# Leaving empty places out of gather and store, and storing expert rows by token

## The chip, the cores and the metric

The kernel runs on one core of one Trainium2 chip. The metric is the device time of one execution in microseconds (us). All tensors are float32.

## The reference

A two layer backbone (D_MODEL 1024) runs over 128 context tokens and 256 latent tokens, 384 in all. Each layer has attention, a recurrent branch, and a mixture of experts (MoE). Only the last is touched by the change:

```python
scores = jax.nn.sigmoid(t.astype(F32) @ router_w.astype(F32))     # 16 experts in 4 groups
...                                                               # best group, top 2 experts in it
_, e_idx = lax.top_k(jnp.where(in_grp, sel, -jnp.inf), TOP_K)
...
gates = jnp.sum(jax.nn.one_hot(e_idx, N_EXPERTS, dtype=F32) * w_sel[..., None], axis=1)
gu = jnp.einsum('td,edf->tef', t, w_gate_up)                      # (1024, 2*512) per expert
g_, u_ = jnp.split(gu, 2, axis=-1)
act = jax.nn.silu(g_) * u_ * gates[..., None].astype(t.dtype)
return jnp.einsum('tef,efd->td', act, w_down).reshape(B, S, D)    # (512, 1024) per expert
```

Every token picks two of 16 experts, so there are 768 pairs of token and pick in a layer, 48 for an expert on average. The result of a token is the sum over its two picks, each scaled by its gate.

## The kernel before

Five engines run instruction streams of their own, written out by hand and tied by semaphores (`S(name)`). SyncE (SP) issues all weight loads in the order of `CHUNKS`. ScalarE (ACT), VectorE (DVE), TensorE (PE) and GpSimd (POOL) each follow the same order of work.

**Routing.** When a layer's attention part is over, the normalized rows of all tokens are stored to `h2_rows` in DRAM. VectorE works out for each pair of token and pick its expert's block (`blk`) and its row in the block (`row`, 0 to CAP-1 with CAP = 128). `hot_c` is the one-hot of the row, `hot_b` the one-hot of the block times the token's number. TensorE multiplies the two (L748), which gives `ids`: for each place of each block the token that sits in it. Empty places hold 0, so they gather row 0. There are 16 blocks, one for each expert, and MORE = 5 blocks for experts with more than 128 rows. In the runs here no such block is needed; its branches are tested and passed over.

**The expert stage.** POOL gathers 128 rows of `h2_rows` for expert e into `xg[e % 2]` (L1878, an indirect DMA); from e = 2 it first waits until the rows of expert e-2 have been turned. TensorE turns them (`xturn`, L756), ScalarE and VectorE copy them as a high and a low part (L1178, L1756). The weights of an expert come in six pieces of 1 MiB (L446), four for gate and up, two for down. ScalarE makes the high part of a piece (`piece_high`, L1173) and VectorE the low part (`piece_low`, L1750, a subtraction of two SBUF tensors). TensorE multiplies them in `split_piece` (L785), 12 matmuls a piece. Its order in an iteration is

```python
gu(e)            # 48 matmuls
xturn(e + 1)     # needs row_gathered of e + 1
dn(e - 1)        # 24 matmuls
aturn(e)         # turns the activated rows, L822
```

ScalarE copies the result of expert e-2 out of PSUM into `yo` (`copy_y`, L1197) in iteration e, after it has made piece 3 of gate and up, and issues the plain store of its 128 rows to `expert_rows` (`store_y`, L1202). `yo` has two buffers.

**The tail.** When the last stores have landed, ScalarE signals `experts_done`. POOL then gathers the rows of each token and pick back (L1903): three tiles of 128 tokens, two picks, six indirect DMAs of 512 KB, with the places `posu = blk * 128 + row`. TensorE adds the two picks of a tile with diagonal matrices of gates (`combined`, L867). SP waits until all six are back (`back{t}`) before it goes on to the next layer's weights.

**The start.** VectorE clears `zrow`, and POOL stores it five times to the rows of the extra blocks (L1851), since the combining gather may name any row. ScalarE issues some 25 small loads; L936 is the last of them, and its first computation (L940) follows.

Of the kernel before, what the change touches and what calls it, by code (L numbers as in the profile page):

```python
# [7 lines left out]
F32 = mybir.dt.float32  # L8
F32R = mybir.dt.float32r
U32 = mybir.dt.uint32  # L10
# [22 lines left out]
CAP = 128  # L33

# [140 lines left out]
def build(nc, x_prompt, x_sample, cache_k, cache_v, state_h, c, c_ctx, norm1_g, norm2_g, w_ada, b_ada,  # L175
# [4 lines left out]
    with ctx:  # L180
# [44 lines left out]
        tokid = con[:, 1174:1177]  # L225
        num_e = con[:, 1177:1193]
        num_b = con[:, 1193:1193 + BLOCKS]
        num_c = con[:, 1193 + BLOCKS:1193 + BLOCKS + CAP]
        sel_e = con[:, 1193 + BLOCKS + CAP:1193 + BLOCKS + CAP + NE]
# [72 lines left out]
        zrow = gbf[:, 2048:3072]  # L302
# [15 lines left out]
        yd = nc.dram_tensor("expert_rows", (BLOCKS * CAP, D), F32, kind="Internal").ap()  # L318
# [18 lines left out]
        def t_free(g):  # L337
            return S(f"tbank_read{T_AT[g] % 2}")
# [69 lines left out]
        def _(sy):  # L408
# [9 lines left out]
            def more_blocks(l):  # L418
# [3 lines left out]
                for b in range(MORE):  # L422
                    with sy.If(more > b):
# [6 lines left out]
                        sy.wait_ge(S(f"x_y_ready{l}"), b + 1)  # L430
                        row = (NE + b) * CAP
                        sy.dma_start(yd[row:row + CAP, :], yo[0][0:CAP, :]).then_inc(S(f"x_stored{l}"), 16)
# [3 lines left out]
                sy.nop().then_inc(S("blocks_over"), 1)  # L436

            for n, (l, name) in enumerate(CHUNKS):
# [467 lines left out]
        def _(ac):  # L906
# [56 lines left out]
            for l in range(DEPTH):  # L963
# [243 lines left out]
                for e in range(NE):  # L1207
# [7 lines left out]
                    if e >= 2:  # L1215
                        store_y(e - 2)
# [13 lines left out]
                store_y(NE - 2)  # L1230
                copy_y(NE - 1)
                store_y(NE - 1)
# [61 lines left out]
        def _(ve):  # L1294
# [11 lines left out]
            ve.memset(zrow, 0.0)  # L1306
# [95 lines left out]
            for l in range(DEPTH):  # L1402
# [20 lines left out]
                def low_part(at):  # L1423
# [3 lines left out]
                    if l == 0 and at == 2:  # L1427
                        ve.wait_ge(S("rows_zero"), 16 * MORE)
# [292 lines left out]
                for i in range(2 * TT):  # L1721
                    pick, t = divmod(i, TT)
                    ins = ve.tensor_scalar(hot_b[:, i, :], num_b, blk[:, pick, t:t + 1], tokid[:, t:t + 1],
                                           ALU.is_equal, ALU.mult)
                ins.then_inc(S("hot_ready"), 1)
                link(ve.scalar_tensor_tensor(posu[:, :, :], blk, float(CAP), row, ALU.mult, ALU.add))
# [232 lines left out]
```

## Time and profile before

| | us |
|---|---|
| median of 3 runs | 1651.53 |
| lowest, highest | 1651.22, 1652.94 |
| the profiled execution | 1651.6 |
| its span | 1649.4 |
| TensorE busy | 1504.6 (91%) |
| VectorE busy | 1111.5 (67%) |
| ScalarE busy | 913.8 (55%) |
| GpSimd busy | 147.5 (9%) |

The span runs from the first to the last recorded instruction; the execution's own time has 2.2 us more around it. Busy times are shares over stages with different limits. The expert stages lie at about 514 to 820 us (layer 0) and 1309 to 1616 us (layer 1). Start times in the views are counted from the start of the span.

### The profile page before, as it was taken

What the parts mean: (1) busy time and instruction counts of PE and PEld (TensorE: products, weight loads), DVE (VectorE), ACT (ScalarE), POOL (GpSimd) and SP (SyncE); (2) the same over time, 40 slices, a digit from 0 to 9 for tenths busy, and PEclk for the clock granted to TensorE, in tenths of its full rate; (3) what the DMA queues carried; (4) which work ended last, traced back from release to release, by engine and by line L of the source; (5) the groups of instructions that cost most, each with busy time, mean ns of one, the idle gap of its engine ahead of it and who ended that gap; (6) DMA issues with size and microseconds to landing.
All of it is one profiled execution on the core that took longest, in us unless ns stands there. A gap on an engine that the chain in (4) does not pass through costs nothing.

```text
span 1649.4 us, 19719 instructions
## 1 busy us (share of the span) xinstructions
PE 1504.6 (91%) x7483; PEld 1219.5 (74%) x7483; DVE 1111.5 (67%) x1715; ACT 913.8 (55%) x1149; POOL 147.5 (9%) x214
## 2 busy tenths in 40 slices
PE   4899999989995999999859999998998499999996
PEld 2499876669864788888657988665988378888876
DVE  3436657764546999999652565766564679999983
ACT  1223569972222787778521345899221467877771
POOL 0100012200011100000040000221000200000001
PEclk9799999989996999999979999999999699999998
DMA  9455432225554999999463554113341589999963
GB/s 345 153 201 196 172 106 83 89 68 189 204 209 168 361 402 407 411 410 397 180 233 109 204 195 163 60 60 107 103 153 48 226 295 409 410 408 406 411 265 131
DMA packets 133876, 377.23 MB, mean 229 GB/s; under 512 B 9352, under 2 KB 12816, under 8 KB 133776
## 3 DMA queue, kind: packets, MB, share of 16 engines
q1 hardware_dynamic: 113600, 326.04, 52.7%
q0 software_dynamic: 11152, 27.80, 4.6%
q10 hardware_dynamic: 9024, 22.03, 3.4%
q8 instruction: 65, 1.06, 0.3%
q14 instruction: 35, 0.29, 0.1%
HBM read 351.19 MB, written 24.66 MB: 228 GB/s over the span
## 4 chain that ended last, share of the span: by engine, by line
PE 83%; DVE 8%; ACT 4%; issue 2%; ACTq 1%; POOL 1%; DMA 0%; DVEq 0%; POOLq 0%
PE bank L785 33%; PE bank L496 23%; PE bank L485 10%; PE bank L506 3%; PE bank L679 2%; PE bank L867 2%; PE bank L756 1%; PE bank L522 1%; PE bank L515 1%; PE bank L652 1%; PE bank L589 1%; PE bank L584 1%; PE bank L822 1%; POOL hT L1858 1%; DVE hyb L1400 1%
## 5 line engine op out<-in xcount | busy, mean ns | idle before, releaser
L785 PE MATMUL bank<-piece_high,ga_r 128*128 128x512 f32 x1536 | 492.8, 402 | 11.7 <-DVE ga_r L1756 7.8
L1750 DVE TENSOR_TENSOR spot_low<-spot,piece_high 128x2048 fp32r<-128x2048 f32 x192 | 435.8, 2288 | 44.1 <-ACT piece_high L1173 40.4
L1173 ACT ACTIVATE piece_high<-spot 128x2048 fp32r<-128x2048 f32 x192 | 367.1, 1917 | 51.7 <-PE bank L785 50.5
L785 PEld LDWEIGHTS bank<-piece_high,ga_r 128*128 128x128 f32 x1536 | 288.4, 191 | 77.2 <-DVE ga_r L1756 9.1
L785 PE MATMUL bank<-spot_low,ga_r 128*128 128x512 f32 x768 | 305.5, 398 | 0.0
L485 PE MATMUL bank<-hT,ring 128*128 128x384 f32 x576 | 196.3, 495 | 19.4 <-POOL hT L1858 12.1
L496 PE MATMUL bank<-parts_r,ga_r 128*128 128x384 f32 x768 | 202.7, 345 | 0.0
L485 PEld LDWEIGHTS bank<-hT,ring 128*128 128x128 f32 x576 | 108.5, 193 | 90.8 <-issue 20.0
L785 PEld LDWEIGHTS bank<-spot_low,ga_r 128*128 128x128 f32 x768 | 146.5, 191 | 34.1
L496 PEld LDWEIGHTS bank<-parts_r,ga_r 128*128 128x128 f32 x768 | 138.3, 188 | 5.9 <-issue 5.0
L496 PE MATMUL bank<-parts_r,gb_r 128*128 128x384 f32 x384 | 129.7, 338 | 0.0
L496 PE MATMUL bank<-parts_r,hT_r 128*128 128x384 f32 x432 | 98.3, 354 | 9.0 <-DVE parts_r L1421 9.0
L1431 DVE TENSOR_TENSOR gb_r<-ring,ga_r 128x1024 fp32r<-128x1024 f32 x48 | 58.5, 1222 | 51.5 <-ACT ga_r L979 49.9
L496 PEld LDWEIGHTS bank<-parts_r,hT_r 128*128 128x128 f32 x432 | 80.6, 197 | 12.7 <-DVE parts_r L1421 10.8
L1878 POOL DMA_INDIRECT gr<-h_rows,ids x32 | 42.5, 1330 | 485.7 <-PE bank L756 435.4
L979 ACT ACTIVATE hT_r<-ring 128x1024 fp32r<-128x1024 f32 x32 | 33.9, 1058 | 77.4 <-PE bank L496 77.4
L1871 POOL DMA_DIRECT2D gatew<-in_lru_wa x64 | 33.8, 534 | 478.6 <-PE bank L679 478.4
L496 PEld LDWEIGHTS bank<-parts_r,gb_r 128*128 128x128 f32 x384 | 72.1, 188 | 0.0
L1178 ACT ACTIVATE ga_r<-bank 128x1024 fp32r<-128x1024 f32 x32 | 32.9, 1027 | 42.8 <-PE bank L756 42.8
L949 ACT ACTIVATE tmp<-bank 128x512 f32<-128x512 f32 x24 | 14.4, 599 | 75.0 <-PE bank L506 75.0
L1858 POOL TENSOR_SCALAR hT<-hT,modA,modT 128x128 f32<-128x128 f32 x32 | 23.3, 744 | 364.1 <-DVE hT L1407 312.5
L506 PE MATMUL bank<-ring,cpad 128*32 128x512 f32 x384 | 51.1, 656 | 0.0
(283 smaller groups left out, 2227.1 us busy)
## 6 DMA issues: line engine op xcount, KB each, us to landing
spot<-in_w_gate_up SPq DMA_DIRECT2D x128, 1024.0 KB, 8.0
spot<-in_w_down SPq DMA_DIRECT2D x64, 1024.0 KB, 8.1
ring<-in_w_ada SPq DMA_DIRECT2D x24, 2048.0 KB, 8.2
ring<-in_w_in SPq DMA_DIRECT2D x22, 2048.0 KB, 8.0
expert_rows<-gb ACTq DMA_DIRECT2D x32, 512.0 KB, 7.0
ring<-in_w_attn_proj SPq DMA_DIRECT2D x4, 2048.0 KB, 8.3
ring<-in_w_rnn_proj SPq DMA_DIRECT2D x4, 2048.0 KB, 7.9
ring<-in_w_out SPq DMA_DIRECT2D x4, 2048.0 KB, 7.9
```

The costliest lines, as they stand in the source:

```text
L485: mm = pe.matmul(bank[:, 0:width], slot_kn(slot)[:, k, n * P:(n + 1) * P], rhs(k), start=(k == 0), stop=(k == KT - 1))
L496: mm = pe.matmul(bank[:, 0:T], w[:, k, :], x[:, k, :], start=(k == 0 and i == 0), stop=(k == KT - 1 and i == 2))
L506: mm = pe.matmul(bank[g:g + 32, :], cpad[:, k, :], slot_kn(s)[:, k, :], start=(k < 4), stop=(k >= 4), tile_position=(0, g))
L679: pe.matmul(bank[:, 0:CW], gatew[:, which, n % 2, :], xc[:, j, :], start=True, stop=True).then_inc(S("gemm_done"), 1)
L785: mm = pe.matmul(out[n], x[:, 2 * q + k, :], w[:, k, cols], start=(q == 0 and k == 0 and i == 0), stop=(q == pieces - 1 and k == 1 and i = ...
L979: ac.activation(w_part(kind, n)[0], slot_kn(s)[:, :, n % 4 * P:(n % 4 + 1) * P], ACT.Copy)\
L1173: ac.activation(highs[p % HIGHS], spots[u], ACT.Copy).then_inc(S("piece_high"), 1)
L1431: ve.tensor_tensor(low, slot_kn(s)[:, :, n % 4 * P:(n % 4 + 1) * P], high.bitcast(F32), ALU.subtract)\
L1750: ve.tensor_tensor(spots_low[u], spots[u], highs[p % HIGHS].bitcast(F32), ALU.subtract)\
L1858: po.tensor_scalar(hT[:, k, 0:CTX], hT[:, k, 0:CTX], modA[:, which, k, 0:1], modT[:, which * 24 + k, 0:1], ALU.mult, ALU.add).then_inc(S(" ...
L1871: po.dma_start(gatew[half * 64:half * 64 + 64, which, n % 2, half * 64:half * 64 + 64], w[l, d, 2 * j + half]).then_inc(S(f"gatew_loaded{n ...
L1878: po.indirect_dma_start(out=dst, out_offset=None, in_=h2d[:, :], in_offset=bass.IndirectOffsetOnAxis(ap=idx, axis=0)).then_inc(sem, 16)
```

## The change

- `rowid` takes the place of `tokid`: for pick 0 the token's number, for pick 1 the number plus 384, both less NOWHERE = 1024. The product of the one-hots then gives these for places in use and 0 for empty ones. Adding 1024 gives a row number of `picked_rows` or, for an empty place, 1024. VectorE makes two tables of it: `ids[:, 1]` for the store, and `ids[:, 0]` for the gather, from which `second` takes 384 away for rows of pick 1.
- Gathers name `ids[:, 0]` with `bounds_check=T - 1`: places past it are left out, and their rows of `xg` keep what was there.
- The result of an expert is stored by an indirect DMA on POOL (`scatter_y`), to row `pick * 384 + token` of `picked_rows`; empty places are left out. ScalarE's plain stores go. In POOL's order the scatter of expert e-2 stands behind the gather of expert e.
- In the tail SP reads the rows back with six plain loads of 128 rows, after `experts_done`, and does not wait for them before the next weights.
- The clearing of the extra rows, and the waits on it, go.

```diff
-        tokid = con[:, 1174:1177]
+        rowid = con[:, 1174:1180]
...
-        posu = sb("posu", [P, 2, TT], U32)
-        ids = sb("ids", [P, BLOCKS], U32)
+        ids = sb("ids", [P, 2, BLOCKS], U32)
+        second = sb("second", [P, BLOCKS])
...
-        yd = nc.dram_tensor("expert_rows", (BLOCKS * CAP, D), F32, kind="Internal").ap()
+        yd = nc.dram_tensor("picked_rows", (2 * T, D), F32, kind="Internal").ap()
@@ SyncE
-                sy.nop().then_inc(S("blocks_over"), 1)
+                sy.wait_ge(S("experts_done"), l + 1)
+                for t in range(TT):
+                    for pick in range(2):
+                        row = pick * T + t * P
+                        sy.dma_start(yg[t][pick], yd[row:row + P, :]).then_inc(S(f"back{t}"), 16)
...
-                    if l + 1 < DEPTH:
-                        for t in range(TT):
-                            sy.wait_ge(S(f"back{t}"), 32 * (l + 1))
@@ ScalarE
-                def store_y(e):
-                    n = l * NE + e
-                    ac.wait_ge(S("y_copied"), n + 1)
-                    ac.dma_start(yd[e * CAP:(e + 1) * CAP, :], yo[e % 2][0:CAP, :]).then_inc(S(f"y_stored{e % 2}"), 16)
@@ VectorE
-            ve.memset(zrow, 0.0)
...
-                    if l == 0 and at == 2:
-                        ve.wait_ge(S("rows_zero"), 16 * MORE)
...
-                link(ve.scalar_tensor_tensor(posu[:, :, :], blk, float(CAP), row, ALU.mult, ALU.add))
-                ve.nop().then_inc(S("places_known"), 1)
                 bank = t_ready(ve, (l, "ids", 0))
-                ve.tensor_copy(ids[0:CAP, :], bank[0:CAP, 0:BLOCKS]).then_inc(t_free((l, "ids", 0)), 1)
+                if l:
+                    ve.wait_ge(S("experts_done"), l)
+                link(ve.tensor_scalar(second[:, :], bank[:, 0:BLOCKS], float(T - NOWHERE), -float(T), ALU.is_ge, ALU.mult))
+                ve.scalar_tensor_tensor(ids[:, 0, :], bank[:, 0:BLOCKS], float(NOWHERE), second[:, :], ALU.add, ALU.add)
+                ve.tensor_scalar(ids[:, 1, :], bank[:, 0:BLOCKS], float(NOWHERE), None, ALU.add)\
+                    .then_inc(t_free((l, "ids", 0)), 1)
@@ GpSimd
-            for b in range(MORE):
-                row = (NE + b) * CAP
-                po.dma_start(yd[row:row + CAP, :], zrow[0:CAP, :]).then_inc(S("rows_zero"), 16)
...
+                def scatter(src, block, sem):
+                    po.indirect_dma_start(out=yd[:, :], in_=src, in_offset=None,
+                                          out_offset=bass.IndirectOffsetOnAxis(ap=ids[:, 1, block:block + 1], axis=0),
+                                          bounds_check=2 * T - 1, oob_is_err=False).then_inc(sem, 16)
+
+                def scatter_y(e):
+                    po.wait_ge(S("y_copied"), l * NE + e + 1)
+                    scatter(yo[e % 2], e, S(f"y_stored{e % 2}"))
 
                 for e in range(NE):
                     n = l * NE + e
                     if e >= 2:
                         po.wait_ge(S("x_turned"), n - 1)
-                    gather(xg[e % 2][0:CAP, :], ids[0:CAP, e:e + 1], S(f"row_gathered{e % 2}"))
+                    gather(xg[e % 2], e, S(f"row_gathered{e % 2}"))
+                    if e >= 2:
+                        scatter_y(e - 2)
+                scatter_y(NE - 2)
+                scatter_y(NE - 1)
...
-                for t in range(TT):
-                    for pick in range(2):
-                        po.indirect_dma_start(out=yg[t][pick], out_offset=None, in_=yd[:, :],
-                                              in_offset=bass.IndirectOffsetOnAxis(ap=posu[:, pick, t:t + 1], axis=0))\
-                            .then_inc(S(f"back{t}"), 16)
```

## Rows read from the trace of the kernel before

**Rows 1.** Busy time by stretches, expert stage; stretch, its length, busy per engine, clock, DMA, GB/s.

```profile
620.00:680.00 60.00, 60.00 (x284) 49.23 (x283) 55.12 (x33) 47.03 (x34) 3.79 (x4) 1.00 1.02 409
```

**Rows 2.** Order of time on POOL: start, duration, what, idle before and releaser.

```profile
520.64 2.78 POOL L1878 DMA_INDIRECT gr<-h_rows,ids  x1 [4.20 <-PE bank L756]
...
553.86 2.61 POOL L1878 DMA_INDIRECT gr<-h_rows,ids  x1 [13.79 <-PE bank L756]
571.85 1.24 POOL L1878 DMA_INDIRECT gr<-h_rows,ids  x1 [15.38 <-PE bank L756]
589.86 1.23 POOL L1878 DMA_INDIRECT gr<-h_rows,ids  x1 [16.78 <-PE bank L756]
```

**Rows 3.** Order of time on VectorE beside these gathers; x2 and x4 are merged neighbours.

```profile
518.12 4.49 DVE L1750 TENSOR_TENSOR spot_low<-spot,piece_high 128x2048 fp32r<-128x2048 f32 x2
...
546.77 8.89 DVE L1750 TENSOR_TENSOR spot_low<-spot,piece_high 128x2048 fp32r<-128x2048 f32 x4
...
569.98 2.29 DVE L1750 TENSOR_TENSOR spot_low<-spot,piece_high 128x2048 fp32r<-128x2048 f32 x1 [0.27 <-ACT piece_high L1173]
```

**Rows 4.** Order of time in one iteration of the expert stage, layer 0.

```profile
705.97 1.02 ACT L1197 ACTIVATE gb<-bank 128x1024 f32<-128x1024 f32 x1
706.11 2.29 DVE L1750 TENSOR_TENSOR spot_low<-spot,piece_high 128x2048 fp32r<-128x2048 f32 x1 [0.33 <-ACT piece_high L1173]
...
708.83 2.29 DVE L1750 TENSOR_TENSOR spot_low<-spot,piece_high 128x2048 fp32r<-128x2048 f32 x1 [0.43 <-ACT piece_high L1173]
...
711.26 2.29 DVE L1750 TENSOR_TENSOR spot_low<-spot,piece_high 128x2048 fp32r<-128x2048 f32 x1
...
714.60 1.04 PE L756 MATMUL bank<-con,gr 128*128 128x128 f32 x8
```

**Rows 5.** Issue to landing: first two gathers, those of 520.64, 553.86, 571.85; small loads.

```profile
DMA to landing us min/median/max: 4.2/4.6/5.0
...
DMA to landing us min/median/max: 5.9/5.9/5.9
...
DMA to landing us min/median/max: 6.4/6.4/6.4
...
DMA to landing us min/median/max: 7.6/7.6/7.6
...
gatew<-in_lru_wa POOLq DMA_DIRECT2D x64, 16.0 KB, 1.9
```

**Rows 6.** TensorE behind waits, and undisturbed (715.63): chain pieces, and order of time.

```profile
715.63 5.57 PE bank L785 x24
...
1334.65 12.95 PE bank L785 x48
...
1607.62 0.71 PE L785 MATMUL bank<-piece_high,ga_r 128*128 128x512 f32 x2 [1.94 <-issue]
...
1607.62 7.36 PE bank L785 x24
```

**Rows 7.** The start: order of time, busy time by stretches, landing of the zeros.

```profile
13.31 7.22 ACTq L936 DMA_DIRECT2D sinkb<-in_attn_sink  x1
...
12.00:16.00 4.00, 0.00 (x0) 0.00 (x0) 0.00 (x0) 0.00 (x0) 0.00 (x0) 1.00 1.04 411
...
DMA to landing us min/median/max: 9.3/12.5/15.9
```

**Rows 8.** Order of time on VectorE at the entry of the expert stage.

```profile
513.91 0.16 DVE L1733 TENSOR_SCALAR pt<-pt 1x16 f32<-1x16 f32 x1
514.11 0.16 DVE L1734 TENSOR_REDUCE nrt<-pt 1x1 f32<-1x16 f32 x1
```

**Rows 9.** The tail of layer 1: order of time, and landing of plain stores.

```profile
1620.17 0.94 POOL L1903 DMA_INDIRECT ga<-expert_rows,posu  x1 [0.30 <-issue]
...
1625.36 0.77 PE L867 MATMUL bank<-qT,gr 128*128 128x128 f32 x2 [10.38 <-issue]
...
DMA to landing us min/median/max: 2.6/7.0/15.9
```

More of the change, by code:

```diff
@@ L33 @@
 CAP = 128
+NOWHERE = 1024
 MORE = (2 * T - 1) // CAP
@@ L224, in build @@
         iota_g = con[:, 1170:1174]
-        tokid = con[:, 1174:1177]
[L226 to L229, printed above, removed]
+        rowid = con[:, 1174:1180]
+        num_e = con[:, 1180:1196]
+        num_b = con[:, 1196:1196 + BLOCKS]
+        num_c = con[:, 1196 + BLOCKS:1196 + BLOCKS + CAP]
+        sel_e = con[:, 1196 + BLOCKS + CAP:1196 + BLOCKS + CAP + NE]
         ones = sb("ones", [P, P])
@@ L1846, in _ @@
             po.wait_ge(S("gatew_zero"), 1)
-            po.wait_ge(S("zeroed"), 1)
-            for b in range(MORE):
-                row = (NE + b) * CAP
-                po.dma_start(yd[row:row + CAP, :], zrow[0:CAP, :]).then_inc(S("rows_zero"), 16)
             for l in range(DEPTH):
@@ L1875, in _, with gather @@
                 po.wait_ge(S("h2_stored"), (l + 1) * TT * 16)
-                def gather(dst, idx, sem):
+                def gather(dst, block, sem):
                     po.indirect_dma_start(out=dst, out_offset=None, in_=h2d[:, :],
-                                          in_offset=bass.IndirectOffsetOnAxis(ap=idx, axis=0)).then_inc(sem, 16)
+                                          in_offset=bass.IndirectOffsetOnAxis(ap=ids[:, 0, block:block + 1], axis=0),
+                                          bounds_check=T - 1, oob_is_err=False).then_inc(sem, 16)
+                def scatter(src, block, sem):
[5 more added lines that the diff above has]
+                    scatter(yo[e % 2], e, S(f"y_stored{e % 2}"))
                 for e in range(NE):
@@ L1892, in _ @@
                             po.wait_ge(S(f"x_pe{l}"), 4 * b)
-                        gather(xg[0][0:CAP, :], ids[0:CAP, NE + b:NE + b + 1], S(f"x_gathered{l}"))
+                        gather(xg[0], NE + b, S(f"x_gathered{l}"))
+                        po.wait_ge(S(f"x_y_ready{l}"), b + 1)
+                        scatter(yo[0], NE + b, S(f"x_stored{l}"))
                     with po.Else():
                         po.nop()
-                po.wait_ge(S("experts_done"), l + 1)
-                po.wait_ge(S("blocks_over"), l + 1)
-                po.wait_ge(S("rows_zero"), 16 * MORE)
-                po.wait_ge(S("places_known"), l + 1)
-                for t in range(TT):
-                    for pick in range(2):
-                        po.indirect_dma_start(out=yg[t][pick], out_offset=None, in_=yd[:, :],
-                                              in_offset=bass.IndirectOffsetOnAxis(ap=posu[:, pick, t:t + 1], axis=0))\
-                            .then_inc(S(f"back{t}"), 16)
 _INS = ["x_prompt", "x_sample", "cache_k", "cache_v", "state_h", "c", "c_ctx", "norm1_g", "norm2_g", "w_ada",
@@ L1935, in shape_constants @@
     tok = np.arange(T).reshape(TT, P).T
+    rowid = np.concatenate([tok, tok + T], 1) - NOWHERE
     parts = [ident, rot, np.cos(ang), np.sin(ang), m0, m1, before, sumsel, row(NE - np.arange(NE)),
-             row(NG - np.arange(NG)), tok, row(np.arange(NE)), row(np.arange(BLOCKS)), row(np.arange(CAP)), sel_e]
+             row(NG - np.arange(NG)), rowid, row(np.arange(NE)), row(np.arange(BLOCKS)), row(np.arange(CAP)), sel_e]
     return np.concatenate([np.asarray(p, np.float32) for p in parts], 1)
```

9 lines of the change are left out of this document (1 added, 8 removed).

## The prediction

> **What bounds the kernel.** I read the busy time by stretches first. In the middle of the expert stage TensorE is busy for all of its 60 us at full clock, and the DMA engines are full too, at 409 GB/s [rows 1]. Two engines at their limit, so I asked which one paces: in the order of time there is no idle TensorE between experts, and each gather follows the one before by 589.86 - 571.85 = 18.01 us [rows 2], one expert. Fewer bytes alone therefore give nothing in this stage; they matter only where TensorE waits. The 28 experts after the first two of each layer are paced this way. So the change can gain at three ends (start, entry and tail of each expert stage) and can lose in the middle, if it makes TensorE wait for anything in any of them.
>
> **What it costs in the middle.** Before, the POOL queue holds one gather per expert, issued as soon as the row turn two experts earlier is done: 18 us of slack. Now the store of expert e-2 is a scatter on the same queue, between gather e and gather e+1. It waits for `y_copied`, and gather e+1 stands behind it. Rows e+1 are turned on TensorE directly after the gate and up products of expert e. I place this in one iteration of the trace [rows 4].
>
> 1. The copy of y ends at 705.97 + 1.02 = 706.99, so the scatter starts at about 707.04.
> 2. How long does an indirect issue take? With VectorE idle in its large subtractions the second gather of a tail needs 0.94 us [rows 9]; but the rows show more. The gather of 520.64 took 2.78 and ended at 523.42; the VectorE subtraction L1750 beside it ended at 522.61. The one of 553.86 ended at 556.47, L1750 at 555.66. The one of 571.85 ended at 573.09, L1750 at 572.27 [rows 2, 3]. Three times the end is that of L1750 plus 0.81 to 0.82 us, whatever the start: POOL waits for L1750 and then needs 0.81.
> 3. The scatter meets L1750 of 706.11, which ends at 708.40: it ends at 709.21. The gather follows 0.30 us later, as in the tail [rows 9], at 709.51, and meets L1750 of 708.83, which ends at 711.12; the next begins at 711.26 [rows 4]. If POOL gets in there, the gather's issue ends at 711.93.
> 4. From the end of the issue to landing: 5.9 - 2.78 = 3.1 us with the DMA engines idle (520.64), 6.4 - 2.61 = 3.8 half loaded (553.86), 7.6 - 1.24 = 6.4 in the full stage, all with 128 rows; a small plain POOL load takes 1.9 from its start [rows 5]. An expert now has 768/16 = 48 rows on average. The load of the DMA engines falls from 7.34 MB per 18 us (six weight pieces of 1 MiB, gather and store of 0.5 MiB) to 6.68 MB, about 91%. I take 3.8, nearest to the half loaded row; bounds are 1.4 (small load, less its issue of about 0.5) and 6.4.
> 5. The rows are there at 711.93 + 3.8 = 715.7. TensorE wants them at 714.60 [rows 4]: 1.1 us late. Bounds: no wait at all if landing takes under 2.67, and 3.7 late at 6.4.
> 6. TensorE's clock adds to that. After a wait of 1.94 us, 24 matmuls took 7.36 us where they take 5.57, because the granted clock went to its lower level (1.2 of 2.4 GHz): 1.8 more. In the first expert of layer 1, behind shorter waits, 48 took 12.95 instead of 11.14: 1.8 more again; the same place of layer 0 lost nearly nothing [rows 6]. For waits near 1.1 us I charge a third of it, 0.6.
>
> So 1.7 us for each gather that stands behind a scatter: gathers 3 to 15, 13 in a layer, 26 in all, 44 us. Both bounds stay for the range: 0, and 3.7 + 1.8 = 5.5 each, 143 us.
>
> The Trainium skill (SBUF — State Buffer, "Who interferes with whom") says that a two-input VectorE operation with both inputs in SBUF contends only with what GpSimd reads there. By that rule only the read of the index column waits, and the next L1750 does not hold up the rest; the trace agrees (0.81 us after each release), and the sum stays 44.
>
> **The start.** Five stores of zeros (2.62 MB) go. At 12 to 16 us the DMA engines are full, at 411 GB/s, and the zeros land 9.3 to 15.9 us after issue. ScalarE is held in the issue of its last small load (L936) from 13.31 to 20.53, and everything up to the first layer follows from ScalarE's next instruction [rows 7]. 2.62 MB at 411 GB/s are 6.4 us; the issue can shrink by at most 7.22 less a normal 0.5, 6.7. Not all of the zeros stand ahead of it: I take 5.5 gained, bounds 0 (if the issue is held by its own queue alone) and 6.7. The cleared row and the wait L1428 have cover: VectorE waits there anyway.
>
> **Entry of each expert stage.** VectorE gets one linked and two plain small operations in place of one cast. Linked ones stand 0.20 apart [rows 8], so the gather and VectorE's first subtractions are about 0.3 later, and the first x_low ends that chain: 0.3 lost per layer, 0.6. The scaled one-hots are the same work, and the removed places were computed while TensorE worked. Bounds 0 and 1.
>
> **Tail of each expert stage.** TensorE waits 10.38 us before its first combining matmul [rows 9]; the copy of y takes 1.06 of it with its start (1.02 in [rows 4]), and 9.3 go to the plain store, its landing (2.6 at least), the first two gathers and theirs. New: the scatter's issue (0.94 to 1.24) and landing (1.4 to 3.1 behind it), 2.4 to 4.3; then two plain loads, 2.6 for one, 0.4 for the second issue and 1.28 for its 524 kB at 411 GB/s, 4.3. Sum 6.7 to 8.6 against 9.3: 0.7 to 2.6 gained, I take 1.5, 3 for two. SP's next weights no longer wait for the rows to be back; they are needed 20 us later, so that is worth nothing. ScalarE loses 32 short issues that lay beside TensorE's work: nothing.
>
> **Sum.** +44 - 5.5 + 0.6 - 3 = +36, on 1651.6 (span 1649.4; median of the runs shown 1651.53): 1688 us. Its own range is 1660 to 1715 (waits of 0.6 to 2 us each).
>
> **Rivals.**
> - *No wait in the middle*: the smaller gathers land within 2.67 us of their issue, or POOL's issues are shorter with few rows. For it: a 16 KB load needs 1.4, and half the bytes go. Against: even idle, 128 rows took 3.1, and one DMA engine may carry as many rows as before. It decides at 2.67 us. Time: 1651.6 - 5.5 - 3 + 0.6 = 1644; range 1640 to 1648. Chance 0.30. The Trainium skill (DMA: Bandwidth & Descriptors, "Anatomy of one DMA — SWDGE (gpsimd) path") gives about 2.0 us plus bytes over 436 GB/s; for 48 rows that would be an estimated 2.45 us and would favour this rival. The trace disagrees where it can be asked: 128 rows into idle DMA engines landed 4.2 and 5.0 us after issue [rows 5], against 3.2 by that rule.
> - *POOL misses the gap of 0.14 us* between 711.12 and 711.26. Then its gather waits for L1750 up to 713.55, ends at 714.36 and lands at 718.2: 3.6 late, with the clock 5.4, times 26 is 140: 1782, range 1750 to 1810. For it: the gap is short; four L1750 in a row kept POOL out to the end of the last. Against: POOL had asked 1.6 us before. Chance 0.18. By the skill's SBUF page (same section) whoever starts first keeps the shared pair for its whole instruction; L1750 of 708.83 would then start at 709.21 and end at 711.50, no gap would be left, and this rival follows. No row here shows POOL delaying L1750.
> - *Gains and losses cancel*, or gathers wait a little in a few experts only: 1648 to 1655. Chance 0.07.
> - My forecast has 0.45.
>
> **How the numbers follow.** The likeliest case gives 1688. The range takes in the fast rival and stops short of the upper half of the slow one: 1641 to 1765. 0.2% (3.3 us) is about what a measurement can tell. Faster by more: 0.29; within: 0.08; slower: 0.63.
>
> **What would show it.** Right: TensorE idle before L756 in experts 3 to 15 of both layers, released by a DMA, about 1 us each, and an expert period above 19; POOL issues end 0.81 us behind an L1750; L936 short and the first kv product some 5 us earlier. Wrong: an unchanged period of 18.0, or gathers whose landing is under 2.7 us from the end of their issue. A shorter hold of POOL by L1750, or fewer rows cutting the issue itself, would break steps 2 and 3; an unchanged L936 would break the start.

## The result and the profile after

| | before | after |
|---|---|---|
| time, median of 4 runs each, side by side | 1651.38 us (1648.68 to 1652.94) | 1698.93 us (1695.71 to 1701.51) |
| ratio, 95% interval | | 1.0297 (1.0280 to 1.0315) |
| span of the profiled execution | 1649.4 us | 1699.7 us |
| mean granted clock | 0.954 | 0.954 |

The kernel is slower by 3%. I looked first at the chain of waits, for TensorE alone, over the whole run and then over the middle of each expert stage (columns: in total, times, longest):

```profile
PE bank L754 <- DMA gr<-h_rows,ids: 56.4, 28, 5.6
...
PE bank L754 <- DMA gr<-h_rows,ids: 21.7, 13, 5.5
PE bank L754 <- DMA gr<-h_rows,ids: 23.8, 13, 3.1
```

L754 is the turn of the gathered rows (L756 before). Before, it waited for a DMA twice, at the two entries. Now it waits 28 times: at the entries, and in experts 3 to 15 of both layers, 21.7 + 23.8 = 45.5 us in 26 experts, 1.75 us each. The busy time of the two expert stages, first product to last, after and then before (columns as in [rows 1]):

```profile
515.80:838.80 323.00, 297.58 (x1336) 239.32 (x1336) 261.82 (x158) 219.47 (x155) 53.75 (x28) 0.97 0.83 304
1341.10:1666.00 324.90, 297.32 (x1336) 239.09 (x1336) 262.26 (x157) 219.55 (x154) 53.36 (x28) 0.98 0.84 303
sum 647.90, PE 594.90 PEld 478.41 DVE 524.08 ACT 439.02 POOL 107.12; mean PE 297.45 PEld 239.20 DVE 262.04 ACT 219.51 POOL 53.56
```
```profile
sum 592.80, PE 585.42 PEld 477.06 DVE 518.88 ACT 438.95 POOL 32.94; mean PE 292.71 PEld 238.53 DVE 259.44 ACT 219.47 POOL 16.47
```

The stages grew by 647.9 - 592.8 = 55.1 us. The same 2672 matmuls were busy 594.9 - 585.4 = 9.5 us longer; the other 45.6 are the waits.

The clock is the smaller part of the 9.5. The granted clock fell beside four of the 26 waits, those of 5.52, 4.38, 3.07 and 2.28 us (0.76 from 561 to 575 us, 0.86 from 800 to 812, 0.81 from 1549 to 1558, 0.83 from 1486 to 1496). The kernel with y copied first (below) has 26 such waits too, and at the granted clock of the kernel before, 0.98 in both stages, its matmuls are still busy 592.2 - 585.4 = 6.8 us longer, 0.26 for each wait. One reason can be read off the trace: a matmul in an unbroken row starts 0.23 us behind the one before and overlaps it, while the last one ahead of a wait counts with its whole 0.40 us (703.72 to 704.12). So some 3 us of the 9.5 are left for the clock, an estimate from these two kernels.

GpSimd's busy time tripled, to 107 us, and that is harmless in itself: it is where a queue stands behind it that it costs. One iteration of the middle, in order of engine and time, the counterpart of [rows 4]:

```profile
695.33 1.02 ACT L1195 ACTIVATE gb<-bank 128x1024 f32<-128x1024 f32 x1
...
695.46 2.29 DVE L1739 TENSOR_TENSOR spot_low<-spot,piece_high 128x2048 fp32r<-128x2048 f32 x1 [0.48 <-ACT piece_high L1171]
698.18 4.73 DVE L1739 TENSOR_TENSOR spot_low<-spot,piece_high 128x2048 fp32r<-128x2048 f32 x2 [0.42 <-ACT piece_high L1171]
...
697.14 1.48 POOL L1868 DMA_INDIRECT picked_rows<-gb,ids  x1 [15.45 <-ACT gb L1195]
698.92 2.44 POOL L1863 DMA_INDIRECT gr<-h_rows,ids  x1 [0.30 <-issue]
...
704.95 1.09 PE L754 MATMUL bank<-con,gr 128*128 128x128 f32 x8 [0.83 <-DMA gr<-h_rows,ids]
```

Read it as a chain. GpSimd has been idle 15.45 us, waiting for the copy of y (696.35). Its store (L1868) starts 0.79 us behind that and ends at 698.62, 0.87 us behind the end of the first subtraction (L1739, 697.75). The gather behind it (L1863) ends at 701.36; the pair of subtractions began at 698.18, the first of the two took about 2.29, so this is 0.89 us behind its end. The rows let TensorE go at 704.95, which is 0.83 us after it was ready.

The start and the tails, answering to [rows 7] and [rows 9]:

```profile
12.98 2.39 ACTq L934 DMA_DIRECT2D sinkb<-in_attn_sink  x1
...
54.37 2.26 PE L483 MATMUL bank<-hT,ring 128*128 128x384 f32 x3 [4.28 <-ACT hT L985]
...
502.75 2.72 PE L746 MATMUL bank<-gb 128*128 128x21 f32 x12 [5.83 <-DVE gb L1709]
...
515.88 1.22 PE L783 MATMUL bank<-piece_high,ga_r 128*128 128x512 f32 x2 [2.82 <-DVE ga_r L1745]
...
850.54 0.77 PE L865 MATMUL bank<-qT,gr 128*128 128x128 f32 x2 [11.74 <-DMA ga<-picked_rows]
...
1675.41 0.77 PE L865 MATMUL bank<-qT,gr 128*128 128x128 f32 x2 [9.44 <-DMA ga<-picked_rows]
```

The held issue is 2.39 us where it was 7.22, and the first kv product comes at 54.37 where it was 62.40. The entry, from the product that makes `ids` to the first expert product, is 515.88 - 502.75 = 13.13 us, against 523.80 - 510.89 = 12.91. The tail waits 11.74 and 9.44 us where it waited 10.7 and 10.38.

### The profile page after: what moved, and what is told of

It is laid out like the page before. It is cut to its first block, busy times and chain, and to the rows that moved or that the text cites. A ratio compares the mean times of both kernels' runs of the same rounds, so it can differ in the third digit from the quotient of the medians.

```text
span 1699.7 us, 19769 instructions
## 1 busy us (share of the span) xinstructions
PE 1514.0 (89%) x7483; PEld 1222.1 (72%) x7483; DVE 1115.4 (66%) x1716; ACT 913.8 (54%) x1149; POOL 208.5 (12%) x229
## 4 chain that ended last, share of the span: by engine, by line
PE 66%; DMA 11%; ACT 8%; DVE 7%; issue 4%; POOL 3%; ACTq 1%; POOLq 0%; SPq 0%; DVEq 0%
PE bank L494 23%; PE bank L783 15%; DMA gr<-h_rows,ids 10%; PE bank L483 10%; ACT piece_high L1171 3%; PE bank L504 2%; POOL picked_rows L1868 2%; PE bank L754 2%; PE bank L677 2%; ACT gb L1195 2%; PE bank L865 2%; PE bank L520 1%; PE bank L650 1%; PE bank L513 1%; PE bank L587 1%
## 5 line engine op out<-in xcount | busy, mean ns | idle before, releaser
L783 PE MATMUL bank<-piece_high,ga_r 128*128 128x512 f32 x1536 | 494.0, 403 | 10.7 <-DVE ga_r L1745 6.9
L1739 DVE TENSOR_TENSOR spot_low<-spot,piece_high 128x2048 fp32r<-128x2048 f32 x192 | 436.5, 2290 | 66.6 <-ACT piece_high L1171 62.8
L1868 POOL DMA_INDIRECT picked_rows<-gb,ids x32 | 46.3, 1448 | 537.0 <-ACT gb L1195 537.0
L754 PE MATMUL bank<-con,gr 128*128 128x128 f32 x256 | 39.3, 303 | 56.4 <-DMA gr<-h_rows,ids 56.4
L754 PEld LDWEIGHTS bank<-con,gr 128*128 128x128 f32 x256 | 31.3, 154 | 68.6 <-DMA gr<-h_rows,ids 68.1
L1863 POOL DMA_INDIRECT gr<-h_rows,ids x32 | 70.7, 2210 | 68.9 <-DVE ids L1717 51.6
```

What stands on the lines that cost most here:

```text
L754: mm = pe.transpose(dst_banks[i][:, k * CAP:(k + 1) * CAP], xrows[0:CAP, kk * P:(kk + 1) * P], ident[0:CAP, 0:CAP])
L783: mm = pe.matmul(out[n], x[:, 2 * q + k, :], w[:, k, cols], start=(q == 0 and k == 0 and i == 0), stop=(q == pieces - 1 and k == 1 and i = ...
L1739: ve.tensor_tensor(spots_low[u], spots[u], highs[p % HIGHS].bitcast(F32), ALU.subtract)\
L1863: po.indirect_dma_start(out=dst, out_offset=None, in_=h2d[:, :], in_offset=bass.IndirectOffsetOnAxis(ap=ids[:, 0, block:block + 1], axis=0 ...
L1868: po.indirect_dma_start(out=yd[:, :], in_=src, in_offset=None, out_offset=bass.IndirectOffsetOnAxis(ap=ids[:, 1, block:block + 1], axis=0) ...
```

## The experiments

My theory: the gather is late because it stands behind a store that waits for y. Rivals: the gather's landing has become longer of itself, or the changed traffic loads the DMA engines. Each kernel ran beside the kernel before on one chip: e1, e3, e4 and e5 on one, e2b, e6, e7 and e8 on another. The median of the kernel before was 1651.69 us on both. TensorE's idle time before the row turn is given as a total of the run; some 10 to 11 us of each are the two entries.

| run | time, us | ratio to before (95%) | waits before the turn, us |
|---|---|---|---|
| kernel before | 1651.7 | | 9.5 |
| changed kernel | 1698.9 | 1.0297 (1.0280 to 1.0315) | 56.4 |
| e1_order | 1641.5 | 0.9939 (0.9922 to 0.9955) | 11.1 |
| e3_fullgather | 1715.5 | 1.0380 (1.0353 to 1.0406) | 65.1 |
| e4_copyfirst | 1696.5 | 1.0277 (1.0260 to 1.0295) | 57.1 |
| e5_gatheronly | 1651.5 | 1.0002 (0.9992 to 1.0012) | 10.6 |
| e2b_latezeros | 1645.3 | 0.9958 (0.9946 to 0.9971) | 9.5 |
| e6_twostores | 1848.9 | 1.1201 (1.1182 to 1.1220) | 155.4 |
| e7_orderfull | 1645.2 | 0.9962 (0.9947 to 0.9976) | 10.4 |
| e8_backwait | 1643.6 | 0.9954 (0.9941 to 0.9967) | 11.4 |

**The store one iteration later.** The changed kernel, with

```diff
                     gather(xg[e % 2], e, S(f"row_gathered{e % 2}"))
-                    if e >= 2:
-                        scatter_y(e - 2)
+                    if e >= 3:
+                        scatter_y(e - 3)
+                scatter_y(NE - 3)
                 scatter_y(NE - 2)
                 scatter_y(NE - 1)
```

> The changed kernel with one thing moved: on GpSimd's queue the store of expert e - 2's rows goes out one iteration later, so that the gather of expert e + 1 stands ahead of it and waits for x_turned alone, as before the change. Theory: the 45.5 us that TensorE waited for gathered rows before L754 (26 experts, 1.75 us each) are there because the gather is queued behind a store that waits for y_copied; they go, and the lower clock and the slower products that follow them (about 9 us) go mostly too: 1699 - 45.5 - 5 to 9 = 1644 to 1649 us, no idle over 0.1 us before L754 in experts 3 to 15, and the expert stage of layer 0 (first L783 to last) back from 322.9 to 296 to 299 us. Rival: it is the landing itself that is longer, because the gathers and stores with left-out places load the DMA engines otherwise: then the waits stay above 1 us each and the time above 1680 us.

Measured 1641.5 us. Its waits of TensorE over the whole run, one iteration, and its two expert stages:

```profile
PE bank L754 <- DMA gr<-h_rows,ids: 11.1, 2, 5.6
```
```profile
699.48 1.01 ACT L1195 ACTIVATE gb<-bank 128x1024 f32<-128x1024 f32 x1
...
701.29 1.50 POOL L1868 DMA_INDIRECT picked_rows<-gb,ids  x1 [13.78 <-ACT gb L1195]
703.10 2.42 POOL L1863 DMA_INDIRECT gr<-h_rows,ids  x1 [0.30 <-issue]
```
```profile
sum 592.50, PE 585.15 PEld 476.82 DVE 518.90 ACT 438.94 POOL 104.17; mean PE 292.57 PEld 238.41 DVE 259.45 ACT 219.47 POOL 52.09
```

Only the two entries wait, and the stages take 592.5 us, as before the change. That alone does not refute the rival of the longer landing, since a gather with a period in hand hides one. The landings do. From the start of the issue, in the middle of layer 0, first the kernel before and then this one:

```profile
L1878 POOL DMA_INDIRECT gr<-h_rows,ids x13: 936/1227/2609, 539.1 to 751.9; - x13
...
DMA to landing us min/median/max: 5.6/7.7/8.6
```
```profile
L1863 POOL DMA_INDIRECT gr<-h_rows,ids x12: 1912/2428/2434, 560.0 to 757.1; - x12
...
DMA to landing us min/median/max: 8.0/8.4/9.4
```

The changed kernel's median is 6.2 (shown below), shorter than both, and it is the only one of the three that waits. One thing in my expectation was wrong: the gather does not wait for `x_turned` alone. It still stands behind a store and is issued at the same point of the iteration, with the same two durations. But it is now the gather of one expert further on, whose rows are wanted a period of 18 us later. What was taken away is not the store in front, it is the need to have the rows at once. The buffers allow this: the turn that empties the buffer ended at 691.15, 12 us before.

**The gathers take all places again.**

```diff
-ve.scalar_tensor_tensor(ids[:, 0, :], bank[:, 0:BLOCKS], float(NOWHERE), second[:, :], ALU.add, ALU.add)
+link(ve.scalar_tensor_tensor(second[:, :], bank[:, 0:BLOCKS], float(NOWHERE), second[:, :], ALU.add, ALU.add))
+ve.tensor_scalar(ids[:, 0, :], second[:, :], float(T - 1), None, ALU.min)
...
-                          in_offset=..., bounds_check=T - 1, oob_is_err=False)
+                          in_offset=...)
```

> The changed kernel, but its gathers take all 128 places again: an empty place's index is clamped to token 383, so the rows of empty places hold another token's row in place of nothing, and the gathers carry no bounds check; the stores are unchanged. It asks what leaving places out of the gather is worth. Theory: a left-out place costs a packet all the same, and the gather is late by its place in the queue, so nothing moves: 1695 to 1704 us, wait before L754 1.5 to 2 us per expert, landing within 0.3 us of the changed kernel's 3.5. The bounds check may cost a start about 0.5 us later after a wait (0.78 to 0.86 against 0.28 before); if it is the check that does this, the gather of each layer's first expert starts 0.5 us earlier here, and nothing else moves, since in the middle the gather follows the store without a wait. Rival: the fewer bytes help, and without them the landing grows towards the 5 to 7.6 us that landings of 128 rows took before: wait per expert +1 us or more, 1720 us and above.

Measured 1715.5 us, 16.5 above the changed kernel, between the two expectations. In the profiled executions it is 12.8 (spans of 1712.5 and 1699.7): the waits are 8.7 us longer, 0.33 for each of 26 experts, and TensorE's busy time in the two stages 3.0 (597.86 against 594.90). The landings of the 13 gathers in the middle of layer 0, counted from the start of the issue (min, median, max), for the changed kernel and for this one:

```profile
L1863 POOL DMA_INDIRECT gr<-h_rows,ids x13: 1906/2432/2435, 558.5 to 795.8; - x13
...
DMA to landing us min/median/max: 5.7/6.2/9.7
```
```profile
L1864 POOL DMA_INDIRECT gr<-h_rows,ids x13: 1866/2381/2394, 561.4 to 808.2; - x13
...
DMA to landing us min/median/max: 5.8/7.1/9.2
```

Leaving places out is worth 0.9 us of landing in the median, so "nothing moves" was wrong; it is worth money where the rows are late, and only there. The bounds check shows as well: without it the first gather starts 509.21 - 508.93 = 0.28 us behind `ids`; with it, in the changed kernel, 0.86.

**ScalarE copies y first.**

```diff
-                    piece_high(f"gu{e}", 3)
                     if e >= 2:
                         copy_y(e - 2)
+                    piece_high(f"gu{e}", 3)
```

> The changed kernel; ScalarE copies expert e - 2's product (copy_y) ahead of the last piece of the next weights (piece_high) instead of behind it, two operations of 1.02 us exchanged. y_copied comes 1.0 to 1.9 us earlier, the store's issue then starts in front of the first subtraction L1739 and not inside it. Theory: the wait before L754 is set by the chain y_copied, store, gather; the chain moves 1.0 to 1.7 us earlier, so of 1.75 us per expert 0 to 0.75 stay: 26 x (1.0 to 1.7) = 26 to 44 us less, 1655 to 1673 us. What goes against it: w_high comes 1.0 us later for VectorE, which may cost the products whose weights it prepares; if these are near their time, 26 x up to 1 us of the gain are given back, and 1670 to 1690 us results. Rival (the landing, not the chain, is late): 1695 to 1702 us.

Measured 1696.5 us, 2.4 below the changed kernel; waits 57.1. This is a clear miss for the theory: the time lies in the range of the rival in the expectation, that the landing and not the chain is late. The same iteration, the landings, and the two expert stages (the row of layer 0, and the sum):

```profile
692.46 1.02 ACT L1195 ACTIVATE gb<-bank 128x1024 f32<-128x1024 f32 x1
...
694.28 0.99 POOL L1868 DMA_INDIRECT picked_rows<-gb,ids  x1 [15.75 <-ACT gb L1195]
...
695.32 6.70 DVE L1739 TENSOR_TENSOR spot_low<-spot,piece_high 128x2048 fp32r<-128x2048 f32 x3 [1.40 <-ACT piece_high L1171]
695.58 2.92 POOL L1863 DMA_INDIRECT gr<-h_rows,ids  x1 [0.30 <-issue]
...
704.65 1.09 PE L754 MATMUL bank<-con,gr 128*128 128x128 f32 x8 [1.59 <-DMA gr<-h_rows,ids]
```
```profile
L1863 POOL DMA_INDIRECT gr<-h_rows,ids x13: 2511/2916/2922, 553.6 to 795.9; - x13
...
DMA to landing us min/median/max: 8.5/9.2/9.7
```
```profile
513.80:836.80 323.00, 296.84 (x1336) 238.73 (x1336) 259.47 (x157) 219.33 (x154) 52.90 (x28) 0.98 0.84 304
...
sum 646.00, PE 592.22 PEld 476.36 DVE 519.05 ACT 438.90 POOL 105.74; mean PE 296.11 PEld 238.18 DVE 259.52 ACT 219.45 POOL 52.87
```

The chain did move as meant. TensorE is ready at 704.65 - 1.59 = 703.06, and the gather's issue ends 4.56 us before that (698.50), where it was 2.76 us before (704.12 less 701.36). But from the end of the issue to the landing it now takes 9.2 - 2.92 = 6.3 us in the median, where it took 6.2 - 2.43 = 3.8. The gain of 1.8 us is eaten by 2.5. Both are needed for the wait: the place in the queue leaves the gather a few us, and the landing decides how many of them are used up. So the landing is no constant that can be added to the issue. It belongs to the moment: the kernel before and the one with the store one iteration later, whose gathers are not waited for, had 7.7 - 1.23 = 6.5 and 8.4 - 2.43 = 6.0.

**The gather alone leaves places out.** The kernel before, with `- NOWHERE` in the token numbers, `+ NOWHERE` where `ids` is written, and the bounds check on its gathers.

> The kernel before, with one part of the change: the gather leaves out the empty places (indices past the end, bounds check), everything else (the plain stores, the gathers at the end, the zeroed rows at the start) as before. Theory: the gather waits for x_turned alone and has 6 us in hand, so leaving places out neither gains nor costs in the middle; each layer's first gather is on the path and starts up to 0.5 us later with the check: 1649 to 1654 us, 0 to +0.2% of the kernel before. Rival: the DMA engines are so full in this stage (409 GB/s) that a third to a half less gathered bytes speeds the weight loads on which TensorE waits: 1635 to 1645 us. Rival on the other side: left-out places slow the transfer, and the waits before L756 return here as well: over 1660 us.

Measured 1651.5 us, ratio 1.0002 (0.9992 to 1.0012), waits 10.6 us at the two entries alone. Leaving places out of a gather that has time in hand is worth nothing here, in either direction. The first gather started 509.74 - 508.87 = 0.87 us behind `ids`.

**The zeros later.** The kernel before, with one wait more ahead of GpSimd's five stores of zeros:

```diff
             po.wait_ge(S("zeroed"), 1)
+            po.wait_ge(S("cvec_ready"), 1)
             for b in range(MORE):
```

> The kernel before; GpSimd issues its five stores of zeros (2.62 MB) only after ScalarE's first operation behind its small loads (L940), at about 17 us in place of 3.7 to 6.1 us. Everything else is as before. Theory: these stores fill the DMA engines while ScalarE's last small load (L936) is issued, and hold its issue for 4.8 us (7.22 against 2.39 us in the changed kernel); without them there it is 2.4 us, and ScalarE's next operation and everything behind it comes 5 us earlier. The further 2.9 us by which the changed kernel's first kv product was earlier come with a higher granted clock in that stretch, and may show here or not. 1651.5 - 5 to 8 = 1643.5 to 1646.5 us. Against it: the stores now lie beside the first layer's weight loads and can hold those by 2.62 MB / 411 GB/s = 6.4 us, and VectorE waits for them before L1428: if they land after its time, nothing is gained: 1650 to 1653 us. Rival (L936 is long by its own queue): L936 stays at 7 us, time unchanged.

Measured 1645.3 us, 6.4 less, with all of the zeros still written:

```profile
12.77 2.09 ACTq L936 DMA_DIRECT2D sinkb<-in_attn_sink  x1
...
17.02 2.85 POOL L1852 DMA_DIRECT2D expert_rows<-gb  x5 [15.74 <-ACT cvec L940]
...
57.07 9.30 PE L485 MATMUL bank<-hT,ring 128*128 128x384 f32 x22 [4.04 <-ACT hT L987]
```

The held issue is 2.09 us, and the first kv product 5.3 us earlier (57.07 against 62.40). The place of that product moves by 5 us from one execution to another, though (see the start, below); what stands is the issue, 7.2 and 7.3 us in the two kernels with the zeros at the front and 2.1 to 2.4 in all eight others, and the 6.4 us between the medians. So the start's gain is the time at which these stores run, not their bytes. A one line edit of the kernel before gets what the whole change gets there, as near as the runs can tell.

**One more store ahead of the gather.** The changed kernel, with (for experts 0 to 12)

```diff
                     scatter(yo[e % 2], e, S(f"y_stored{e % 2}"))
+                    if l and e == 0:
+                        po.wait_ge(S("spare_stored"), 16 * (NE - 3))
+                    if e < NE - 3:
+                        po.indirect_dma_start(out=spare[:, :], in_=con[:, 0:D], in_offset=None,
+                                              out_offset=..., bounds_check=2 * T - 1, oob_is_err=False)
```

> The changed kernel with a dose more of the suspected cost: behind the store of each of experts 0 to 12, GpSimd issues one more indirect store with the same indices (constant rows into a tensor that nobody reads), ahead of the gather that waits in its queue. The DMA engines move 6.25% of rows more. Theory: each indirect issue is held by the VectorE subtraction L1739 beside it until it ends and takes 0.88 us from there. The extra store takes the place in which the gather got in (ends 3.04 us after the start of the pair of L1739), and the gather ends 0.88 us after the second L1739: 2.4 us later. TensorE's wait before L754 grows by what the gather is later, 1.2 (if the landing after a later issue is shorter, as the run with copy_y first suggests the other way round) to 2.5 us, in 26 experts: + 31 to 65 us, 1730 to 1764 us, and a further 0 to 20 us by the clock. Rival (place in the queue does not matter, the load of the DMA engines does): rows of 1.3 MB in all per layer are worth 4 us a layer at 409 GB/s, 1707 us at most.

Measured 1848.9 us, 150 above the changed kernel:

```profile
714.66 1.50 POOL L1869 DMA_INDIRECT picked_rows<-gb,ids  x1 [17.37 <-ACT gb L1196]
716.47 2.40 POOL L1879 DMA_INDIRECT spare_rows<-con,ids  x1 [0.30 <-issue]
719.17 2.20 POOL L1864 DMA_INDIRECT gr<-h_rows,ids  x1 [0.30 <-issue]
...
725.74 1.26 PE L755 MATMUL bank<-con,gr 128*128 128x128 f32 x8 [4.08 <-DMA gr<-h_rows,ids]
...
715.73 4.72 DVE L1740 TENSOR_TENSOR spot_low<-spot,piece_high 128x2048 fp32r<-128x2048 f32 x2 [0.43 <-ACT piece_high L1172]
```
```profile
sum 792.90, PE 641.17 PEld 517.21 DVE 525.97 ACT 438.71 POOL 163.32; mean PE 320.58 PEld 258.60 DVE 262.98 ACT 219.36 POOL 81.66
```

The queue works as the theory said: the extra store takes the place between the two subtractions, and the gather ends 0.92 us behind the second (715.73 + 4.72 = 720.45; 721.37). From the copy of y to the gather's end it is 7.48 us (713.89 to 721.37) where it was 5.01: 2.47 more. But the price was twice what I expected. Waits rose by 155.4 - 56.4 = 99.0 us, 3.8 per expert, since the landing behind a third transfer grew too (median 7.9 from the start of an issue of 2.2, 5.7 behind its end). And TensorE's busy time in the stages rose by 641.2 - 594.9 = 46.3 us, at a lower clock: the trace shows the granted clock at its lower level beside each of these 26 waits, 3.8 to 7.9 us long (mean granted clock 0.919 against 0.954; 0.89 and 0.90 in the two stages against 0.97 and 0.98). The load rival (1707 us at most) falls.

**All places again, with the store one iteration later.** Both edits above together.

> The kernel with the store one iteration later (gather e + 1 ahead of the store of e - 2), in which moreover the gathers take all 128 places (empty ones clamped to token 383, no bounds check), so that no gather leaves anything out; the stores still do. In the changed kernel this edit cost 16 us (1715 against 1699 us). Theory: these 16 us came through the late gathers alone (more rows to land after a late issue); where the gather has a whole expert in hand, they vanish: 1640 to 1645 us, within 0.2% of the run with the order alone. The entry of each layer may be 0.5 us shorter by the missing check and up to 1 us longer by 80 more rows in the first gather. Rival: the DMA engines are the bound themselves now that nothing waits, and 16 x 80 rows of 4 KB per layer (5.2 MB, 12.8 us at 409 GB/s) show: 1650 us and above.

Measured 1645.2 us, where the order alone had 1641.5. The intervals (0.9947 to 0.9976 and 0.9922 to 0.9955) overlap. Of the 16.5 us that the edit cost with late gathers at most a few are left. This stands between the theory and its rival; the waits (10.4) say that it is not the middle.

**SyncE waits for the rows at the tail.** The kernel with the store one iteration later, and

```diff
                         sy.dma_start(yg[t][pick], yd[row:row + P, :]).then_inc(S(f"back{t}"), 16)
+                for t in range(TT):
+                    sy.wait_ge(S(f"back{t}"), 32 * (l + 1))
```

> The kernel with the store one iteration later, in which SyncE waits, as it did before the change, until all six loads of the stored rows are back, before it issues the next weights (L449). Theory: in the run with the order alone the first combining matmul of layer 0 still waits 10.6 us, as before the change, because the pair of rows for it (524 kB each) lands 4.4 to 5.2 us after issue, and the next weights stand behind it in the same queues only: nothing is gained at the first pair, 1641 to 1644 us. Rival: the weights issued 3.2 us behind the first load share the DMA engines with the six loads and delay them; then the wait falls by 0.5 to 1.5 us in layer 0 and the whole combining stage by up to 2 us, 1639 to 1641 us. On the other side, the weights themselves come up to 7 us later; if they are needed within 20 us, TensorE waits for them at the next layer's start: 1645 us or more.

Measured 1643.6 us. The tail of layer 0 waits 10.24 us in place of 10.61: next to nothing, as the theory had it. I found no way here to make the tail pay.

## Why the prediction was right

The forecast was 1688 us (1660 to 1715 as its own range); 1699 was measured, by the mechanism that it named: the store in front of the gather, and the gather's short time in hand. That the sum came so near is in part luck, since one of its terms (step 4) was right for a wrong reason. Term by term, in us:

| term | predicted | measured | shown by |
|---|---|---|---|
| middle, waits | +44 with the clock | +45.5 | waits at L754, e1_order |
| middle, longer busy time | (in the 44) | +9.5 | busy time of the stages |
| start, held issue | -5.5 | -5.2 | issue of L934 |
| start, up to the first kv product | (none) | -2.8 | first kv product; this execution |
| entry | +0.6 | +0.2 each | 13.13 against 12.91 |
| tail | -3 | +1.0 and -0.9 | first L865 |

- *Steps 1 to 3* (store and gather each end 0.81 behind a subtraction, and the gather gets in between two): measured 0.87 and 0.89, and the gap was enough. Of the changed kernel's 64 gathers and stores, 56 had a subtraction end inside their issue, and each of them ended 0.86 to 0.90 us behind it. Step 1 had the store start 0.05 behind the copy of y; it is 0.79, which costs nothing as long as the subtraction beside it ends later. It holds even where three subtractions stand without any idle time between them:

```profile
555.02 6.68 DVE L1739 TENSOR_TENSOR spot_low<-spot,piece_high 128x2048 fp32r<-128x2048 f32 x3
...
555.76 2.43 POOL L1868 DMA_INDIRECT picked_rows<-gb,ids  x1 [40.20 <-ACT gb L1195]
558.49 1.91 POOL L1863 DMA_INDIRECT gr<-h_rows,ids  x1 [0.30 <-issue]
```

  The store ends at 558.19 and the gather at 560.40. A third of 6.68 is 2.23, so the subtractions end near 557.3 and 559.5, and each issue ends 0.9 behind one. The rival in which GpSimd misses the gap (1782; its own terms add up to 1784) falls with that. Its support, that four subtractions in a row kept GpSimd out to the end of the last, was a misreading of [rows 2] and [rows 3]: that gather started at 553.86, and the last of the four began at about 553.4, so it was held by one only. Nor does GpSimd push the next subtraction back: the pair beside the gather took 4.73 us, the pair of 708.83 to 713.55 in [rows 4], with no gather beside it, 4.72, and the mean of all 192 is 2.290 us against 2.288 before. The Trainium skill (SBUF — State Buffer, "Who interferes with whom") says of VectorE's two-port modes that whoever issues first gets the shared pair for the whole instruction; the prediction took that over for this subtraction, which reads both its inputs from SBUF. These rows do not bear it out for an indirect issue: the subtraction of 698.18 starts 0.44 us before the store's issue ends.
- *Step 4* (3.8 us from the end of the issue to the landing): 3.8 in the median. The number was right by luck, and the reasoning behind it was not. I took it for a matter of the load, a little under 3.8 for fewer rows. e4_copyfirst shows 6.3 in a kernel with the same rows and the same load over the stage (304 GB/s in both), and e3_fullgather 4.7 with 128 rows.
- *Step 5* (1.1 us late): the wait is 1.75 in the mean, because some gathers landed later than the one I placed. In the iteration above it is 0.83, at the first gather behind a store up to 5.5.
- *Step 6* (0.6 for the clock): wait and longer busy time are 55.1 / 26 = 2.1 us together, where I had 1.7. The busy time is 9.5 / 26 = 0.37 of it, and by e4_copyfirst 0.26 of these come without a lower clock, which leaves some 0.1 for the clock. So two terms were mis-sized, against each other: the wait, at 1.75 for 1.1, and the clock, at 0.1 for 0.6; and the 0.26 by which a break in the row of matmuls costs more than its wait was in no term.
- *The rest of the 50.3 us* by which the span grew (55.1 - 8.0 + 0.4 + 0.1 = 47.6): behind the longer tail of layer 0 the combining matmuls took 1.4 us longer and the first kv products 0.7, beside a granted clock that stayed at its lower level for 13.7 us and not 10.2. No term of the sum had them; the last 0.6 us have no cause that I can name.
- *The entry*: the number was near, but the gather was later by a term that the sum lacked. The bounds check makes it start 0.86 us behind `ids` in place of 0.28. It cost nothing, since the first expert product waits for VectorE (2.82 us, 3.43 before).
- *The start*: the held issue gave 20.53 - 15.37 = 5.2 us, as predicted. The other 2.8 came further on, in the stretch up to the first kv product, where pieces of the same products ran at the higher clock. They belong to this execution and not to the change: from the end of the held issue to the first kv product it is 36.9 to 42.2 us in the ten profiled executions, 41.9 in that of the kernel before and 39.0 in that of the changed one. In e5_gatheronly, whose zeros and held issue (7.33 us) are those of the kernel before, it is 37.0, and the product comes at 57.28, as early as in e2b_latezeros. The granted clock there is at its lower level for 6.8 us from 40.4 on, and in the kernel before for 13.7 us from 41.8 on.
- *The tail*: predicted to gain 1.5 in each, it lost 1.0 and gained 0.9. The store and its landing were sized well enough (840.64 to about 843.8). The pair of plain loads is the term that was mis-sized: 4.3 predicted, 850.54 - 843.84 = 6.7 measured in layer 0. While they run, the DMA engines move 205 to 320 GB/s, not 411.
- *The rival with no wait in the middle* (1644) needed a landing under 2.67 us from the end of the issue. None was in the changed kernel's 26; the shortest took 3.3. Its time is near that of e1_order, 1641.5: this is what the change is worth without the queue. And the 18 us of slack that I gave the gather of the kernel before was one period too few, since its rows are wanted two turns later; it hung on nothing.

Of the 10 us that e1_order is faster than the kernel before, e2b_latezeros explains 6.4, and e5_gatheronly shows that the gathers explain none. The rest, some 4 us of which the tail of layer 1 is 0.8 (9.6 against 10.38), is near what the runs can tell. e1_order is the fastest version found, and the one to keep. What decides whether a landing takes 3.8 or 6.3 us was not settled by a run. The weights are the candidate. In the changed kernel SyncE's four pieces of gate and up had gone out 2.4 us before the end of the gather's issue (698.96 to 701.36); with y copied first, 0.6 us before (697.90 to 698.50). In the kernel before a piece took 8.3 us to land in this stretch, in the changed one 4.9. The traces of the kernel before, the changed one and the six runs that edit the expert stage (all but e2b and e8) bear it out. I counted, for their 256 gathers, the pieces of weights that were issued and had not landed when the gather's issue ended:

| pieces under way | gathers | issue's end to landing, us: median (lowest to highest) |
|---|---|---|
| none | 48 | 3.2 (2.6 to 4.6) |
| one | 47 | 4.2 (3.1 to 6.9) |
| two | 124 | 6.2 (3.8 to 8.2) |
| three or four | 37 | 6.4 (5.2 to 7.3) |

Of the changed kernel's 26 gathers behind a store 18 had one piece under way; with y copied first all 26 had two. That would account for the 3.8 and the 6.3, and for why an earlier issue won nothing; but it is a correlation, and no run changed the pieces alone.

## What to carry to other kernels

When a step moves onto an in-order queue, ask which instruction stands behind it and when that one's result is wanted. If there is a buffer to spare, put the later step first: one place in the order was worth 57 us here, against 10 that the rest of the change saves. Do not count a transfer's landing as a constant while the DMA engines are full, but look at what is under way when it is issued; 1.8 us more in hand at the issue left the wait for the rows as it was. And look at when a useless transfer runs before removing it: moving the zeros by 13 us gave 6.4 us, as near as the runs can tell what leaving them out gives.

## What the runs showed of the hardware

- A place left out of an indirect transfer still shows a packet. In the 38 us from 690 to 728, the changed kernel's four indirect transfers show 576 packets, 144 each, as the full gathers had before, though more than half of all places are empty (768 tokens in 16 blocks of 128) (columns: packets, MB, share of 16 engines); the kernel before had 288 packets and 1.05 MB for two full gathers, and over the same work (690 to 726 us) 257 packets under 512 B against 517.

```profile
q0 software_dynamic: 576, 1.00, 7.2%
```

- A bounds check makes an indirect issue start 0.58 us later behind a wait: 0.86 and 0.87 against 0.28. Behind another issue there is no difference, 0.30 both ways.
- With VectorE's two-input subtractions back to back, an indirect issue of GpSimd still gets in when one of them ends, and ends 0.86 to 0.92 us from there; the subtractions take no longer (2.290 us in the mean against 2.288 in the kernel before).
- The time from the end of an indirect issue to the landing went from 3.8 to 6.6 us in the same stage by the median of 12 or 13 gathers, and from 3.2 to 6.4 by the number of weight pieces under way (table above). The number of rows, 48 on average or 128, is worth 0.6 to 0.9 us: 3.8 against 4.7 in the changed kernel, 6.0 against 6.7 (e7_orderfull) with the store one iteration later, 5.8 (e5_gatheronly) against 6.5 in the kernel before.
- Short waits cost TensorE more than their length. 26 waits that add up to 45.5 us came with 9.5 us of longer busy time, some 3 of it (an estimate) by the clock; 26 waits of 3.8 to 7.9 us came with a further 46.3 us, at a granted clock of 0.89 and 0.90.
